# Up product of a decoder layer: the four sums of each unit's hidden rows on VectorE instead of GpSimd

## Chip, cores and metric

The kernel runs on one core of one Trainium2 chip. The metric is the device time of one launch in microseconds (us), the median over several runs; lower is better.

## What is computed

One layer of a decoder trunk for 2048 prompt tokens and 64 sample tokens (8 sequences of 8), model width 1024, hidden width 4096, all in float32. After the mixer (sparse attention and a gated recurrence) comes the part that matters here:

```
x = x + rmsnorm(mix, g_post_mix)
hid = jnp.square(jax.nn.relu(rmsnorm(x, g_pre_mlp) @ w_up))
x = x + rmsnorm(hid @ w_down, g_post_mlp)
```

The change lies in the product with w_up for the prompt rows and its squared ReLU.

## The kernel before

The launch has three stages: projections, attention, and output with MLP. The last one, `output_and_mlp`, does the output product, then the up product, then the down product. Both MLP products for the prompt use Winograd's form of Strassen's scheme: a product of two 2x2 block matrices is made from seven block products P1 to P7 instead of eight, at the price of sums of blocks before and after. Since a fast fp32r matmul has less precision than float32, each operand is split into a high part (a rounding copy on ScalarE) and a low part (raw minus high, on VectorE), and each block product is three passes: high x high, high x low, low x high.

**The up product.** The prompt is cut into two halves (h = 0, 1) of 1024 tokens. Each half has 16 units (f), each of two columns of blocks of w_up, so there are NU = 32 units of NPROD = 7 products, in the order P1, P2, P6, P5, P7, P3, P4; n = 7u + i numbers the products from 0 to 223. A product is 12 matmuls of 128x128 by 128x512 into one of 8 PSUM banks. Its operand on the side of w_up is one piece of 256 KB per product, its operand on the side of the tokens is four pieces (q) of 256 KB that are loaded once per half, in its first unit (unit 0 and unit 16). So `PIECES` lists five pieces per product for units 0 and 16 and one for all others, and `READY_AT[n]` is the count of pieces that product n needs. The raw pieces pass through RAW = 12 buffers (`up_raw`).

Each engine has its own program and they meet by semaphores:

- **SyncE** (its DMA queue is SP) walks the products. For product n it issues loads until piece READY_AT[n] + 12 (`load_up`; each waits until VectorE has made the low part of the piece 12 back, semaphore `lo_rdy`). At i == 4 of unit u it issues the stores of unit u - 1 (`store_hidden(u - 1)`, L3049): seven DMAs of 256 KB to scratch, after a wait for `hid_rdy` and `hsum_rdy`. Loads and stores are in one queue, in this order of the program.
- **ScalarE** makes high parts AHEAD = 5 products ahead (`up_high`, L3255 for tokens, L3260 for w_up), copies P1 out of its bank (`first_out`, L3267), and makes ReLU and square of the four blocks of hidden rows (`square_hidden`, L3272 and L3274, `hid_rdy`).
- **VectorE** does for each n first the low parts of product n + 5 (`up_low`, L3460) and then takes product n out of its bank with Winograd's sums (`out_of_up_bank`, L3479 to L3493).
- **TensorE** (`up`, L3700) waits for the low parts of product n (`lo_rdy`) and for its bank.
- **GpSimd** (`hidden_sums`, L3163 to L3169) makes from the four squared blocks of a unit the four sums that the down product's seven forms need. The hidden rows of even and odd units lie in two buffers, `hidden_even` and `hidden_odd`.

```
                        if u and i == 4:
                            store_hidden(u - 1)
                sp.wait_ge(hs_out[0], 16 * NPROD * NU // 2)
                for m in range(B_RAW, HALF_K):
                    load_b(m)
```

**Into the down product.** The first four pieces of w_down (`load_b`, L3062) are loaded while the last unit runs; pieces 4 to 7 wait until the stores of unit 30 have landed (the two lines above behind the loop). The first hidden rows (`load_a`, L3178) come over GpSimd's queue. The stores of unit 31 stand in SP ahead of the pieces of w_down for the second group of steps; ScalarE makes the high part of the first of these ahead of the hidden rows of the third down step.

Of the kernel before, what the change touches and what calls it, by code (L numbers as in the profile page):

```python
# [22 lines left out]
ALU = mybir.AluOpType  # L23
# [2776 lines left out]
def output_and_mlp(nc, io, sc):  # L2800
# [30 lines left out]
    with ExitStack() as ctx:  # L2831
# [104 lines left out]
        def H(u):  # L2936
            return H_odd if u % 2 else H_even
# [69 lines left out]
        with nc.Block() as block:  # L3007
# [117 lines left out]
            def _(pool):  # L3125
# [28 lines left out]
                        pool.dma_start(sc["xc"][h, i, :, :, own], sums[:, m % 2, s, :].rearrange("p (q t) -> p q t", q=QUADS))\  # L3154
                            .then_inc(xsum_out[m % 2], 16)

                def hidden_sums(u):
                    z = H(u)
                    a11, a12, a21, a22 = z[:, P1, :], z[:, P2, :], z[:, C12, :], z[:, P4, :]
                    pool.wait_ge(hid_rdy, 4 * u + 3)  # L3160
                    if u >= 2:
                        pool.wait_ge(hs_out[u % 2], 16 * NPROD * (u // 2))
                    pool.tensor_tensor(z[:, P5, :], a21, a22, ALU.add).then_inc(hsum_rdy, 1)  # L3163
                    pool.tensor_tensor(z[:, P7, :], a11, a21, ALU.subtract).then_inc(hsum_rdy, 1)
                    pool.wait_ge(hsum_rdy, 4 * u + 1)
                    pool.tensor_tensor(z[:, P6, :], z[:, P5, :], a11, ALU.subtract).then_inc(hsum_rdy, 1)
                    pool.wait_ge(hid_rdy, 4 * u + 4)
                    pool.wait_ge(hsum_rdy, 4 * u + 3)
                    pool.tensor_tensor(z[:, P3, :], a12, z[:, P6, :], ALU.subtract).then_inc(hsum_rdy, 1)  # L3169

                def load_a(s):
                    i, kk, r = STEPS[s]
                    if s >= A_RAW:
# [21 lines left out]
                for n in range(TILES + 2):  # L3195
                    if n >= 3:
                        forms(n - 2)
                    if n < TILES:
                        store_x1(n)
                for u in range(NU):  # L3200
                    if u == NU - 1:
                        pool.wait_ge(mm_done, LAST_UP - 4)
                        for s in range(A_RAW):
                            load_a(s)
                    hidden_sums(u)
                k = 0
                for s in range(len(STEPS)):
                    if s + A_RAW < len(STEPS):
# [212 lines left out]
            def _(dve):  # L3421
# [30 lines left out]
                def up_low(g):  # L3452
# [6 lines left out]
                        high, out = wp[:, n % SLOTS, 0, :], wp[:, n % SLOTS, 1, :]  # L3459
                    dve.tensor_tensor(out, raw[:, g % RAW, :], high.bitcast(F32), ALU.subtract).then_inc(lo_rdy, 1)  # L3460

                def out_of_up_bank(n):
                    u, i = divmod(n, NPROD)
                    z, h = up_bank(n), H(u)
                    if i == P1:
                        return
                    dve.wait_ge(mm_done, n + 1)
                    if i == P2:
                        dve.wait_ge(s1_rdy, u + 1)
                        if u == 0:  # L3470
                            dve.wait_ge(o_sq, 2 * TILES)
                            for b in range(LOAD):
                                dve.wait_ge(x1_out[b], 16 * len(range(b, TILES, LOAD)))
                        elif u == 1:
                            wait_x_stored(dve, 1)
                        else:
                            dve.wait_ge(hs_out[u % 2], 16 * NPROD * (u // 2))
                            dve.wait_ge(hsum_rdy, 4 * (u - 1))
                        dve.tensor_tensor(h[:, P1, :], s1[:, :], z, ALU.add).then_inc(ev, 1)  # L3479
                    elif i == P6:  # L3480
                        dve.tensor_tensor(u2[:, :], s1[:, :], z, ALU.add).then_inc(ev, 1)
                    elif i == P5:
                        dve.wait_ge(ev, NPROD * u + 2)
                        dve.tensor_tensor(u4[:, :], u2[:, :], z, ALU.add).then_inc(ev, 1)
                    elif i == P7:
                        dve.wait_ge(ev, NPROD * u + 3)
                        dve.tensor_tensor(u3[:, :], u2[:, :], z, ALU.add).then_inc(ev, 1)
                        dve.wait_ge(ev, NPROD * u + 4)
                        dve.tensor_tensor(h[:, P4, :], u3[:, :], up_bank(n - P7 + P5), ALU.add).then_inc(ev, 1)
                    elif i == P3:  # L3490
                        dve.tensor_tensor(h[:, C12, :], u4[:, :], z, ALU.add).then_inc(ev, 1)
                    else:
                        dve.tensor_tensor(h[:, P2, :], u3[:, :], z, ALU.subtract).then_inc(ev, 1)  # L3493
# [113 lines left out]
                for n in range(-AHEAD, len(READY_AT)):  # L3607
                    while n + AHEAD < len(READY_AT) and split < READY_AT[n + AHEAD]:
                        up_low(split)
                        split += 1  # L3610
                    if n >= 0:
                        out_of_up_bank(n)
                    if n == LAST_UP - 3:
                        b_low(0)
                        b_low(1)
                    if n == LAST_UP - 2:
                        for m in range(2, 6):
                            b_low(m)
                        a_low(0)
                    if n == LAST_UP - 1:  # L3620
                        b_low(6)
                        b_low(7)
                        a_low(1)

                k = 0
                for s, (i, kk, r) in enumerate(STEPS):
                    if s == 1:
# [270 lines left out]
```

## Time and profile before

| | |
|---|---|
| median of 3 runs | 4140.19 us (4137.55 to 4142.27) |
| the profiled execution, its own time | 4148.16 us |
| its span in the trace | 4146.4 us |
| TensorE busy | 3604.0 us, 87% of the span |
| VectorE busy | 2882.3 us, 70% |
| ScalarE busy | 2206.5 us, 53% |
| GpSimd busy | 924.2 us, 22% |
| mean granted TensorE clock | 0.931 |
| up product | from about 2796 to 3428 us of the span |

Times in rows of the timeline are us from the start of the span. The profiled execution is 1.8 us longer than its span and 8.0 us above the median. A row of the timeline joins like instructions that follow each other: start, time until the end of the last, engine, line, operation, tiles, count, and in brackets the idle time ahead of it and what ended it.

### The profile page before, as it was taken

The numbers are of one execution on the slowest core, as the hardware profiler recorded it, in microseconds if no ns is written. First come the engines' busy times: TensorE is split into PE (matmuls) and PEld (weight loads), VectorE is DVE, ScalarE is ACT, GpSimd is POOL, SyncE is SP. The second block draws the span as 40 slices with busy tenths as digits, with TensorE's granted clock in tenths as the row PEclk, the third lists the DMA queues.
The fourth block names the chain that finished last, engine by engine and source line by source line (L and its number), as shares of the span: only waits on it lengthen the run. The fifth ranks groups of instructions, "written<-read, shape, count | busy, mean of one in ns | idle before, by whom it ended". The sixth has DMA issues, their size and how long they took to land. (4 is left out here: it accounts for less than half of the span.)

```text
span 4146.4 us, 52837 instructions
## 1 busy us (share of the span) xinstructions
PE 3604.0 (87%) x18060; PEld 2870.5 (69%) x18061; DVE 2882.3 (70%) x4890; ACT 2206.5 (53%) x3666; POOL 924.2 (22%) x945
## 2 busy tenths in 40 slices
PE   8999997778877479875399998878999998999998
PEld 7878776667755235444288886767887886888886
DVE  6685665887798788888578885666556554564565
ACT  3343333655677589887477774335455443443232
POOL 0000002554311011100156640343222331000011
PEclk9999998999977799996599999989999999999999
DMA  6555444334300134432456643457668656554464
GB/s 171 170 145 161 137 126 116 94 96 131 92 26 26 51 132 166 160 112 94 133 174 223 224 147 115 163 188 235 197 189 257 194 175 197 181 187 150 137 215 135
DMA packets 487214, 624.48 MB, mean 151 GB/s; under 512 B 97432, under 2 KB 329848, under 8 KB 478648
## 3 DMA queue, kind: packets, MB, share of 16 engines
q1 hardware_dynamic: 424584, 361.25, 29.5%
q0 software_dynamic: 61968, 260.07, 18.6%
q8 instruction: 137, 2.24, 0.2%
q14 instruction: 109, 0.89, 0.1%
q10 hardware_dynamic: 416, 0.02, 0.0%
HBM read 444.45 MB, written 176.77 MB: 150 GB/s over the span
## 5 line engine op out<-in xcount | busy, mean ns | idle before, releaser
L3700 PE MATMUL up_acc<-x_parts_first,w_up_parts 128*128 128x512 f32 x1536 | 357.5, 392 | 26.3 <-DVE w_up_parts L3460 26.3
L712 PE MATMUL accumulated<-hT,w_in_parts 128*128 128x512 f32 x1536 | 356.7, 392 | 0.0
L3700 PEld LDWEIGHTS up_acc<-x_parts_first,w_up_parts 128*128 128x128 f32 x1536 | 290.6, 189 | 87.8 <-DVE w_up_parts L3460 27.2
L2710 DVE TENSOR_SCALAR_CACHE_REDUCE junk_dve<-score,candidate 128x2048 bf16<-128x2048 f32 (+6 forms) x224 | 328.5, 1505 | 8.8 <-DVE candidate L2696 8.3
L3791 PE MATMUL down_acc<-w_down_parts_even,hidden_parts 128*128 128x512 f32 x1344 | 316.4, 393 | 17.8 <-DVE hidden_parts L3497 11.6
L712 PEld LDWEIGHTS accumulated<-hT,w_in_parts 128*128 128x128 f32 x1536 | 288.2, 189 | 60.8
L3791 PE MATMUL down_acc<-w_down_parts_odd,hidden_parts 128*128 128x512 f32 x1344 | 312.7, 390 | 0.0
L3791 PEld LDWEIGHTS down_acc<-w_down_parts_even,hidden_parts 128*128 128x128 f32 x1344 | 254.7, 190 | 72.2 <-issue 19.0
L2633 ACT ACTIVATE junk_act<-score,candidate 128x1920 bf16<-128x1920 f32 (+6 forms) x224 | 285.9, 1287 | 21.0 <-DVEq L2697 16.4
L3791 PEld LDWEIGHTS down_acc<-w_down_parts_odd,hidden_parts 128*128 128x128 f32 x1344 | 251.8, 188 | 53.2 <-issue 1.0
L330 ACT ACTIVATE w_in_parts<-w_in_raw 128x1024 fp32r<-128x1024 f32 (+1 forms) x112 | 113.6, 1014 | 308.9 <-PE accumulated L708 121.7
L3280 ACT ACTIVATE hidden_parts<-hidden_raw 128x1024 fp32r<-128x1024 f32 x112 | 118.6, 1059 | 288.8 <-PE down_acc L3791 288.8
L468 DVE TENSOR_TENSOR w_in_parts<-w_in_raw,w_in_parts 128x1024 fp32r<-128x1024 f32 (+1 forms) x112 | 130.9, 1169 | 195.2 <-ACT w_in_parts L330 194.3
L3460 DVE TENSOR_TENSOR w_up_parts<-up_raw,w_up_parts 128x512 fp32r<-128x512 f32 x224 | 176.8, 789 | 115.0 <-ACT w_up_parts L3260 113.4
L708 PE MATMUL accumulated<-w_in_parts,hT 128*128 128x512 f32 (+1 forms) x1152 | 239.1, 366 | 1.7 <-DVE hT L489 1.7
L2018 DVE TENSOR_TENSOR probs_T<-p_T,probs_T 128x512 fp32r<-128x512 f32 x272 | 183.8, 688 | 76.0 <-ACT probs_T L1939 74.9
L708 PEld LDWEIGHTS accumulated<-w_in_parts,hT 128*128 128x128 f32 x1152 | 200.3, 188 | 31.4 <-issue 1.9
L1296 PE MATMUL dots<-ki_high,qi_parts 128*128 128x512 f32 (+3 forms) x304 | 145.8, 481 | 71.9 <-ACT relu L1318 70.0
L3497 DVE TENSOR_TENSOR hidden_parts<-hidden_raw,hidden_parts 128x1024 fp32r<-128x1024 f32 x112 | 137.0, 1223 | 101.8 <-ACT hidden_parts L3280 101.4
L1939 ACT ACTIVATE probs_T<-p_T 128x512 fp32r<-128x512 f32 x272 | 157.1, 594 | 94.1 <-PE p_T L1876 93.0
L3764 PE MATMUL out_acc<-w_out_parts,mix_T 128*128 128x512 f32 (+1 forms) x816 | 196.2, 400 | 2.0 <-DVE w_out_parts L3578 2.0
L1365 DVE SCALAR_TENSOR_TENSOR score<-relu,wi,score 128x1024 f32<-128x1024 f32 (+7 forms) x154 | 180.4, 1172 | 24.9 <-ACT relu L1318 7.9
(535 smaller groups left out, 8534.2 us busy)
## 6 DMA issues: line engine op xcount, KB each, us to landing
hidden_raw<-scratch_hs POOLq DMA_DIRECT2D x112, 512.0 KB, 4.6
w_in_raw<-in_w_in SPq DMA_DIRECT2D x80, 512.0 KB, 4.1
up_raw<-scratch_ws SPq DMA_DIRECT2D x128, 256.0 KB, 4.1
scratch_hs<-hidden_even SPq DMA_DIRECT2D x112, 256.0 KB, 3.6
scratch_hs<-hidden_odd SPq DMA_DIRECT2D x112, 256.0 KB, 3.7
up_raw<-in_w_up SPq DMA_DIRECT2D x96, 256.0 KB, 4.7
weight_sums<-in_w_down POOLq DMA_DIRECT2D x16, 1024.0 KB, 5.3
scratch_wt<-weight_sums POOLq DMA_DIRECT2D x16, 1024.0 KB, 5.6
```

Source lines behind the costliest of these rows:

```text
L708: mm = pe.matmul(z, h[:, a, k, n * P:(n + 1) * P], w2[:, g % 2, b, k2 * w:(k2 + 1) * w], start=(first and j == 0), stop=(last and j == 2))
L712: mm = pe.matmul(z, w2[:, g % 2, b, k2 * ST + n * P:k2 * ST + (n + 1) * P], h[:, a, k, :], start=(first and j == 0), stop=(last and j == 2))
L1296: pe.matmul(dots[:, u % DB, c:c + w], qs[:, b, h, :], kh[:, k], start=True, stop=False)
L1365: dve.scalar_tensor_tensor(s, r, wi[:, i, h:h + 1], s, ALU.mult, ALU.add).then_inc(acc_done, 1)
L1939: act.activation(ET[:, s % 3, 0, :], pT[:, turn_at[s] % 3, :], ACT.Copy).then_inc(th_rdy, 1)
L2018: dve.tensor_tensor(ET[:, s % 3, 1, :], pT[:, turn_at[s] % 3, :], ET[:, s % 3, 0, :].bitcast(F32), ALU.subtract).then_inc(tl_rdy, 1)
L2633: act.activation(ja[:, n % 2, 0:WIDTH[i]], score[:, SOFF[i]:SOFF[i + 1]], ACT.Sign, bias=cf[:, c:c + 1], accum_out=cnt[:, c:c + 1]).then_i ...
L2710: dve.tensor_scalar(jd[:, n % 2, 0:WIDTH[i]], score[:, SOFF[i]:SOFF[i + 1]], cf[:, c:c + 1], None, ALU.is_ge, ALU.add, accum_out=cnt[:, c: ...
L3460: dve.tensor_tensor(out, raw[:, g % RAW, :], high.bitcast(F32), ALU.subtract).then_inc(lo_rdy, 1)
L3700: mm = pe.matmul(up_bank(n), wp[:, n % SLOTS, b, q * P:(q + 1) * P], X(i)[:, a, q, :], start=(q == 0 and (a, b) == (0, 0)), stop=(q == QUA ...
L3764: mm = pe.matmul(acc[0:rows(n), n % 2, c, :], aT[:, n % 2, a, k, 0:rows(n)], wo[:, k, b, c * ST:(c + 1) * ST], start=(k == 0 and (a, b) == ...
L3791: mm = pe.matmul(down_bank(s), ap[:, s % A_PARTS, a, j * P:(j + 1) * P], B(ph)[:, j, b, :], start=(j == 0 and (a, b) == (0, 0)), stop=(j = ...
```

## The change

`hidden_sums` moves from GpSimd's program into VectorE's, with the same four operations, semaphores and waits. VectorE calls it for unit u - 1 right behind the eviction of P5 of unit u (n % 7 == 3), and for the last unit, 31, behind the whole loop. GpSimd keeps only its loads of hidden rows at that place. ScalarE, TensorE and SP have the same instructions in the same order as before.

```diff
@@ gpsimd
-                def hidden_sums(u):
-                    z = H(u)
-                    a11, a12, a21, a22 = z[:, P1, :], z[:, P2, :], z[:, C12, :], z[:, P4, :]
-                    pool.wait_ge(hid_rdy, 4 * u + 3)
-                    if u >= 2:
-                        pool.wait_ge(hs_out[u % 2], 16 * NPROD * (u // 2))
-                    pool.tensor_tensor(z[:, P5, :], a21, a22, ALU.add).then_inc(hsum_rdy, 1)
-                    pool.tensor_tensor(z[:, P7, :], a11, a21, ALU.subtract).then_inc(hsum_rdy, 1)
-                    pool.wait_ge(hsum_rdy, 4 * u + 1)
-                    pool.tensor_tensor(z[:, P6, :], z[:, P5, :], a11, ALU.subtract).then_inc(hsum_rdy, 1)
-                    pool.wait_ge(hid_rdy, 4 * u + 4)
-                    pool.wait_ge(hsum_rdy, 4 * u + 3)
-                    pool.tensor_tensor(z[:, P3, :], a12, z[:, P6, :], ALU.subtract).then_inc(hsum_rdy, 1)
@@ gpsimd
-                for u in range(NU):
-                    if u == NU - 1:
-                        pool.wait_ge(mm_done, LAST_UP - 4)
-                        for s in range(A_RAW):
-                            load_a(s)
-                    hidden_sums(u)
+                pool.wait_ge(mm_done, LAST_UP - 4)
+                for s in range(A_RAW):
+                    load_a(s)
@@ vector
+                def hidden_sums(u):
...
+                    dve.tensor_tensor(z[:, P5, :], a21, a22, ALU.add).then_inc(hsum_rdy, 1)
...
@@ vector
                     if n >= 0:
                         out_of_up_bank(n)
+                    if n >= NPROD and n % NPROD == P5:
+                        hidden_sums(n // NPROD - 1)
@@ vector
+                hidden_sums(NU - 1)
                 k = 0
                 for s, (i, kk, r) in enumerate(STEPS):
```

The first place is VectorE from the low parts of product 112 on, where the token pieces of the second half begin (unit 15). Before:

```order
L3460 TENSOR_TENSOR x_parts_first<-up_raw,x_parts_first 128x512 x4
L3460 TENSOR_TENSOR w_up_parts<-up_raw,w_up_parts 128x512
L3484 TENSOR_TENSOR sum_four<-sum_two,up_acc 128x512
L3460 TENSOR_TENSOR x_parts_first<-up_raw,x_parts_first 128x512 x4
L3460 TENSOR_TENSOR w_up_parts<-up_raw,w_up_parts 128x512
L3487 TENSOR_TENSOR sum_three<-sum_two,up_acc 128x512
```

In the changed kernel (L3443 is L3460 of before, L3481 is L3484, L3484 is L3487):

```order
L3443 TENSOR_TENSOR x_parts_first<-up_raw,x_parts_first 128x512 x4
L3443 TENSOR_TENSOR w_up_parts<-up_raw,w_up_parts 128x512
L3481 TENSOR_TENSOR sum_four<-sum_two,up_acc 128x512
L3451 TENSOR_TENSOR hidden_even<-hidden_even 128x512
L3452 TENSOR_TENSOR hidden_even<-hidden_even 128x512
L3454 TENSOR_TENSOR hidden_even<-hidden_even 128x512
L3457 TENSOR_TENSOR hidden_even<-hidden_even 128x512
L3443 TENSOR_TENSOR x_parts_first<-up_raw,x_parts_first 128x512 x4
L3443 TENSOR_TENSOR w_up_parts<-up_raw,w_up_parts 128x512
L3484 TENSOR_TENSOR sum_three<-sum_two,up_acc 128x512
```

Unit 14's sums now stand on VectorE behind the eviction of P5 of unit 15, and the low parts of product 114 (the second row of x_parts_first) stand behind them. The same pattern stands in each of the units 1 to 31.

The second place is VectorE at the end of the up product, in the changed kernel (L3490 takes the last product out of its bank):

```order
L3490 TENSOR_TENSOR hidden_odd<-sum_three,up_acc 128x512
L3451 TENSOR_TENSOR hidden_odd<-hidden_odd 128x512
L3452 TENSOR_TENSOR hidden_odd<-hidden_odd 128x512
L3454 TENSOR_TENSOR hidden_odd<-hidden_odd 128x512
L3457 TENSOR_TENSOR hidden_odd<-hidden_odd 128x512
L3500 TENSOR_TENSOR w_down_parts_odd<-down_raw,w_down_parts_odd 128x512
```

The sums of unit 31 stand between the last eviction and the first low part for the second group of down steps; before, these two followed each other.

## Rows read from the trace of the kernel before

**Rows 1.** The page: the span, and the median landing of hidden stores.
```profile
span 4146.4 us, 52837 instructions
...
scratch_hs<-hidden_odd SPq DMA_DIRECT2D x112, 256.0 KB, 3.7
```

**Rows 2.** Waits of TensorE, 2787 to 3600 us: us in total, times, longest.
```profile
PE up_acc L3700 <- DVE w_up_parts L3460: 31.5, 5, 16.9
```

**Rows 3.** Windows: length, then busy us of PE, PEld, DVE, ACT, POOL; PEclk, DMA.
```profile
3150.00:3169.00 19.00, 19.00 (x85) 15.73 (x84) 14.04 (x18) 11.75 (x21) 10.85 (x8) 1.00 0.87 253
...
3135.00:3142.30 7.30, 7.30 (x25) 5.92 (x26) 5.99 (x10) 1.79 (x3) 0.00 (x0) 0.77 1.00 283
```

**Rows 4.** Groups of the up stage, busy and mean ns; then L3460, 3127 to 3135 us, min/median/max.
```profile
L3163 POOL TENSOR_TENSOR hidden_even<-hidden_even 128x512 f32<-128x512 f32 x16 | 20.7, 1294 | 212.2 <-ACT hidden_even L3274 212.2
...
L3484 DVE TENSOR_TENSOR sum_four<-sum_two,up_acc 128x512 f32<-128x512 f32 x32 | 22.0, 686 | 35.3 <-PE up_acc L3700 35.3
...
L3460 DVE TENSOR_TENSOR x_parts_last<-up_raw,x_parts_last x5: 679/1757/1779, 3127.8 to 3134.8; 128x512 fp32r<-128x512 f32 x5
```

**Rows 5.** Timeline of an ordinary odd-even pair of units, 3160 to 3185 us.
```profile
3161.14 11.04 PE L3700 MATMUL up_acc<-x_parts_first,w_up_parts 128*128 128x512 f32 x48
...
3167.40 5.49 SPq L3049 DMA_DIRECT2D scratch_hs<-hidden_odd  x7
...
3172.22 0.69 DVE L3484 TENSOR_TENSOR sum_four<-sum_two,up_acc 128x512 f32<-128x512 f32 x1 [1.17 <-PE up_acc L3700]
```

**Rows 6.** Timeline of unit 15 and the start of unit 16, 3103 to 3128 us.
```profile
3104.92 5.04 SPq L3049 DMA_DIRECT2D scratch_hs<-hidden_even  x7
...
3109.53 2.49 DVE L3460 TENSOR_TENSOR x_parts_first<-up_raw,x_parts_first 128x512 fp32r<-128x512 f32 x4
...
3110.00 2.70 SPq L3037 DMA_DIRECT2D up_raw<-scratch_xc  x4
...
3112.53 0.68 DVE L3484 TENSOR_TENSOR sum_four<-sum_two,up_acc 128x512 f32<-128x512 f32 x1
...
3115.28 2.59 ACT L3255 ACTIVATE x_parts_first<-up_raw 128x512 fp32r<-128x512 f32 x4 [4.89 <-DMA up_raw<-scratch_xc]
...
3117.81 11.04 PE L3700 MATMUL up_acc<-x_parts_first,w_up_parts 128*128 128x512 f32 x48
...
3118.57 0.69 DVE L3460 TENSOR_TENSOR w_up_parts<-up_raw,w_up_parts 128x512 fp32r<-128x512 f32 x1
```

**Rows 7.** Timeline of unit 16 and the start of unit 17, 3127 to 3146 us.
```profile
3127.84 6.45 DVE L3460 TENSOR_TENSOR x_parts_last<-up_raw,x_parts_last 128x512 fp32r<-128x512 f32 x4
...
3134.95 7.31 PE L3700 MATMUL up_acc<-x_parts_last,w_up_parts 128*128 128x512 f32 x24 [3.38 <-DVE w_up_parts L3460]
...
3139.16 2.71 SPq L3042 DMA_DIRECT2D up_raw<-scratch_ws  x4
...
3141.00 0.68 DVE L3484 TENSOR_TENSOR sum_four<-sum_two,up_acc 128x512 f32<-128x512 f32 x1
...
3143.93 0.69 DVE L3460 TENSOR_TENSOR w_up_parts<-up_raw,w_up_parts 128x512 fp32r<-128x512 f32 x1 [2.25 <-ACT w_up_parts L3260]
```

**Rows 8.** Timeline from the up to the down product, 3414 to 3460 us.
```profile
3414.80 9.28 SPq L3049 DMA_DIRECT2D scratch_hs<-hidden_even  x7
...
3419.74 0.69 DVE L3484 TENSOR_TENSOR sum_four<-sum_two,up_acc 128x512 f32<-128x512 f32 x1 [2.03 <-PE up_acc L3700]
...
3427.65 1.76 SPq L3062 DMA_DIRECT2D down_raw<-scratch_wt  x4
...
3434.10 13.38 PE L3791 MATMUL down_acc<-w_down_parts_even,hidden_parts 128*128 128x512 f32 x48 [6.24 <-issue]
...
3437.08 0.68 DVE L3493 TENSOR_TENSOR hidden_odd<-sum_three,up_acc 128x512 f32<-128x512 f32 x1
...
3442.46 7.78 SPq L3049 DMA_DIRECT2D scratch_hs<-hidden_odd  x7
...
3458.77 4.85 PE L3791 MATMUL down_acc<-w_down_parts_even,hidden_parts 128*128 128x512 f32 x12 [11.30 <-DVE hidden_parts L3497]
```

More of the change, by code:

```diff
@@ L3460, in up_low @@
                     dve.tensor_tensor(out, raw[:, g % RAW, :], high.bitcast(F32), ALU.subtract).then_inc(lo_rdy, 1)
+                def hidden_sums(u):
+                    z = H(u)
+                    a11, a12, a21, a22 = z[:, P1, :], z[:, P2, :], z[:, C12, :], z[:, P4, :]
+                    dve.wait_ge(hid_rdy, 4 * u + 3)
+                    if u >= 2:
+                        dve.wait_ge(hs_out[u % 2], 16 * NPROD * (u // 2))
+                    dve.tensor_tensor(z[:, P5, :], a21, a22, ALU.add).then_inc(hsum_rdy, 1)
+                    dve.tensor_tensor(z[:, P7, :], a11, a21, ALU.subtract).then_inc(hsum_rdy, 1)
+                    dve.wait_ge(hsum_rdy, 4 * u + 1)
+                    dve.tensor_tensor(z[:, P6, :], z[:, P5, :], a11, ALU.subtract).then_inc(hsum_rdy, 1)
+                    dve.wait_ge(hid_rdy, 4 * u + 4)
+                    dve.wait_ge(hsum_rdy, 4 * u + 3)
+                    dve.tensor_tensor(z[:, P3, :], a12, z[:, P6, :], ALU.subtract).then_inc(hsum_rdy, 1)
                 def out_of_up_bank(n):
```

## The prediction

> **What bounds the kernel now.** The page gives the span [rows 1]; the change touches only the up product and the step into the down product, so I read TensorE's waits there first. In the whole up stage it waits for a low part five times, 31.5 us in all, 16.9 of them at its start [rows 2]. Elsewhere it is never idle: in an ordinary window of one unit's length it is busy 19.00 of 19.00 us at full clock, VectorE 14.04 and GpSimd 10.85 [rows 3]. So per unit the bound is TensorE, seven products of 2.72 us (48 matmuls of four products take 11.04 us, [rows 5]), and VectorE has room. What can move the time are places where something is late already: the change of halves at unit 16, where TensorE stood 3.38 us for a low part [rows 7], and the step into the down product, where it stood 6.24 and 11.30 us [rows 8]. At each of them I follow SP, because SP keeps its program order and the moved sums release its stores.
>
> **Cost on VectorE.** Added are 128 operations (4 x 32) of 128x512. GpSimd took 1294 ns for such a one; an operation of VectorE on that shape takes 686 ns, its source in PSUM or not [rows 4], and four in a row 2.49 us [rows 6]. With one link of dependence I take 2.6 us a unit. Nominal work of VectorE per unit is then 14 x 0.69 + 2.6 = 12.3 us of 19: covered by TensorE, and low parts are made five products (13.6 us) ahead. If this cover failed, each us would cost 30 us in all; it is a rival below.
>
> **Gain on VectorE.** Where the sums on GpSimd ran beside low parts, a low part took 1757 ns instead of 679 [rows 4]: at unit 16 four of them took 6.45 us [rows 7] instead of 2.49 [rows 6], and TensorE's 3.38 us stall follows on that. The Trainium skill (SBUF — State Buffer, Who interferes with whom) says that a VectorE operation with two SBUF inputs and a GpSimd operation that reads SBUF exclude each other on one shared port for the whole instruction; these rows agree. By that rule alone the change removes a stall, and that is a rival.
>
> **What the later sums do to SP.** Here I part from it. In an ordinary unit the stores of the unit before begin 6.3 us into the unit (3167.40 against 3161.14, [rows 5]). Now the sums come behind the eviction of P5, 3172.22 + 0.7, plus 2.6: 3175.5, so the stores start 8.1 us later, and all loads behind them too. In an ordinary unit that is hidden: with 12 buffers the piece behind the stores is first read about 30 us into the unit (it belongs to product 7u + 17, whose high part may be written once product 7u + 10 is through, 11 x 2.72 us), and it would land 14.4 + 5.5 + about 5 = 25 us into it. The stores themselves land at 14.4 + 5.5 + 3.7 [rows 1], 23 us in, before the same buffer is written again at 24.5.
>
> At the change of halves it isn't hidden, since there 12 buffers are only 2.4 products.
>
> *Stores of unit 14.* SP has loaded through product 113 when it comes to them; product 114's token pieces stand behind. Before: stores at 3104.92, loads at 3110.00, ScalarE reads at 3115.28 after 4.89 us of waiting for them, last low part ready at 3118.57 + 0.69 = 3119.26 [rows 6]. TensorE needs it two products after 3117.81, at 3123.25: 4.0 us of room. Now: eviction of P5 at 3112.53, sums from about 3112.7 to 3115.3, stores then, 10.4 us later. Everything behind is a chain, load by load, so product 114 is ready at 3129.7: a stall of 6.4 us. Products 115 to 118 come at the pace of their loads and high parts, each later than TensorE by about 1 us; TensorE is through with 118 at about 3148, where it was at 3142.26 before.
>
> *Stores of unit 15.* SP stands at product 116 and has loaded through 120; 121 is behind the stores. Before: its load at 3139.16, its low part ready at 3143.93 + 0.69 = 3144.62 [rows 7], needed at 3147.55 (two products after 3142.10). Now the sums follow the eviction of P5, which was at 3141.00 [rows 7]. It comes 10.4 us later by the chain and 2.7 earlier because the four low parts no longer take 6.45 us (4.0 less, of which 1.3 goes to waiting for ScalarE): 3148.7, sums done 3151.9, seven stores of about 5.4 us, load at 3157.35, and from there 5.46 us as before: 3162.8. TensorE restarts 15.2 us later than before. It stood 9 us before that, and after a stall it runs slowly: after the 3.38 us stall 24 matmuls took 7.31 us at a granted clock of 0.77, that is 1.2 GHz for part of it [rows 7, 3], against 5.6 (half of 11.04 and the tail of the last), 1.7 us lost. The two new stalls each pay this; the first is absorbed by the second. **Term one: 15.2 + 1.7 = +17 us**; as bounds I take 13 (loads that land faster once nothing else runs) and 20.
>
> The Trainium skill (Perfetto Trace Analysis, DMA Optimizations) advises one DMA-capable engine for inputs and another for outputs; it speaks against a change that makes outputs late in a queue of inputs. In this kernel rows 6 already show a load waiting behind stores.
>
> **The step into the down product.** Stores of unit 30 were issued at 3414.80 and the pieces of w_down that wait for their landing at 3427.65, 12.85 us later [rows 8]. Now the sums follow 3419.74: done at 3423.0, 8.2 us later. But the stores ran beside 2.5 MB of first loads (9.28 us to issue instead of 5.5); 8 us later these are over, and issue plus landing should be 5.5 + 3.7 - 0.7 = 8.5 us: pieces at 3431.5, +3.8, and TensorE's restart too, from 3434.10 to 3437.9. Its two steps of 13.38 us end at 3451.3, still inside the next stall. That one hangs on the sums of unit 31: GpSimd ended them at 3442.4 (the stores start at 3442.46, [rows 8]); VectorE starts after its eviction, 3437.08 + 3.8 + 0.6, and ends at 3444.1: +1.7. The stores then took 7.78 us beside two loads of hidden rows, which GpSimd, now free, issues earlier: I take 6.5, between 5.5 and 7.78, so w_down's pieces and the restart of 3458.77 come 0.4 us later. **Term two: +0.4 us**, bounds -0.6 and, with stores of unit 30 that take 12.85 us again, +6.
>
> **Sum.** 17.0 + 0.4 = +17.4 us. Against the profiled execution's 4148.2 us that is 4165.6; it stands 8.0 above the median, so against 4140.2 it gives **4157.6 us**, 0.42% slower. About 0.2%, 8.3 us, is what a measurement can tell from no change.
>
> **Rivals.**
>
> *The port wins, not slower (4133 us).* If product 114's pieces still come in time, TensorE loses nothing there, and the stall of 3.38 us with its 1.7 goes: -5.1; at the end unit 31's sums take 2.6 instead of 5.3 us, about -2. It decides at a delay of the stores of under 4.0 us at unit 15. For it: low parts of 1757 ns. Against: SP's order is unchanged, ScalarE already waits 4.89 us for that load, and my delay is 10.4. Chance 0.07, by a third of it faster than 0.2%, were the port worth more elsewhere.
>
> *Only the second store binds (4147 us).* If the loads behind unit 14's stores catch up (they were issued without waiting, and could land faster), 121 is ready 10.4 us earlier, at 3152.4, 4.9 us after its need, plus 1.7 and 0.4: +7. Against: the chain from load to low part has no slack in rows 6. Chance 0.10.
>
> *The end isn't softened (4162 us).* Unit 30's stores take 12.85 us again: +4.4 more. For: SP issues at a pace that I only infer from other units. Chance 0.17.
>
> *VectorE waits in every unit (about 4187 us).* The buffer of hidden rows is free 23 us into a unit and written at 24.5; a landing some us late stops VectorE and with it the low parts. It would have to eat 11 us of lead. One us per unit is 30 us. Chance 0.04.
>
> *As forecast:* 0.62, its own range 4152 to 4162.
>
> **Range and chances.** 4147 to 4165 takes in the forecast, the third rival, the bounds of both terms and the edge of the second rival. Slower by over 0.2%: 0.62 + 0.17 + 0.04 and 0.02 of the second rival, 0.85. Within 0.2%: 0.08 of the second and 0.05 of the first, 0.13. Faster: 0.02.
>
> **What the profile of the changed kernel would show.** Ordinary windows of 19 us with TensorE busy throughout, VectorE about 12.3, and no low part above 0.7 us: right on the cover and the port. The stores of unit 14 at about 3115 us and a TensorE stall of 6 us two products into unit 16; a second of 9 us two products into unit 17, both behind a load of up_raw; a granted clock under 1 behind each. A restart of the down product about 4 us later relative to the last up matmul, and the next at the same distance as before. I am wrong if the loads of product 114 are issued ahead of the stores or land with room, if the stall stays one of 3 us, or if TensorE has gaps in ordinary units.

## The result, and the profile after

The changed kernel takes 4157.81 us (median of 6 runs, 4150.89 to 4159.79); the kernel before took 4142.47 in the same comparison (6 runs, 4137.55 to 4147.01). The ratio is 1.0035, 95% interval 1.0022 to 1.0048: 15.3 us slower by the medians, 14.5 by the ratio. The forecast was 4157.6, +17.4.

The page of the changed kernel, the parts that answer to [rows 1] and the shares of the engines:

```profile
span 4155.9 us, 52838 instructions
...
PE 3608.8 (87%) x18061; PEld 2872.2 (69%) x18061; DVE 2930.8 (71%) x5018; ACT 2205.2 (53%) x3666; POOL 743.7 (18%) x817
...
L3443 DVE TENSOR_TENSOR w_up_parts<-up_raw,w_up_parts 128x512 fp32r<-128x512 f32 x224 | 154.0, 688 | 139.0 <-ACT w_up_parts L3243 138.9
```

The same group on the page of the kernel before:

```profile
L3460 DVE TENSOR_TENSOR w_up_parts<-up_raw,w_up_parts 128x512 fp32r<-128x512 f32 x224 | 176.8, 789 | 115.0 <-ACT w_up_parts L3260 113.4
```

The low parts take 688 ns each over all 224 pieces of weights, where they took 789. The gain that the sums' leaving was to bring VectorE is there: with 128 operations more, of 0.69 us each, it is busy only 48.5 us longer (2930.8 against 2882.3). TensorE nevertheless waits longer for the low parts. What TensorE waits for in the up product and the step behind it (the view of [rows 2]; us in total, times, longest):

```profile
PE up_acc L3700 <- DVE w_up_parts L3443: 44.5, 7, 16.0
PE down_acc L3791 <- issue: 9.3, 1, 9.3
PE down_acc L3791 <- DVE hidden_parts L3494: 6.1, 2, 5.8
```

44.5 us against 31.5, while the last of the three, 11.30 us at its longest in [rows 8], is down to 5.8. An ordinary window of one unit, and the first stall at the change of halves (columns as in [rows 3]):

```profile
3200.00:3219.00 19.00, 19.00 (x86) 15.73 (x85) 11.48 (x18) 9.27 (x18) 0.00 (x0) 1.00 0.67 200
3125.00:3134.00 9.00, 8.34 (x26) 6.42 (x27) 8.96 (x15) 8.78 (x16) 0.00 (x0) 0.70 1.05 394
```

TensorE is busy 19.00 of 19.00 us with GpSimd at zero and VectorE at 11.48: the added work costs nothing there. At the change of halves something isn't covered. This is TensorE's own timeline from unit 15 on (start, length, then in brackets the idle time before it):

```profile
3094.09 11.04 PE L3700 MATMUL up_acc<-x_parts_first,w_up_parts 128*128 128x512 f32 x48
...
3125.66 7.97 PE L3700 MATMUL up_acc<-x_parts_first,w_up_parts 128*128 128x512 f32 x24 [6.92 <-DVE w_up_parts L3443]
...
3144.04 5.60 PE L3700 MATMUL up_acc<-x_parts_first,w_up_parts 128*128 128x512 f32 x24
3157.96 7.18 PE L3700 MATMUL up_acc<-x_parts_first,w_up_parts 128*128 128x512 f32 x24 [8.32 <-DVE w_up_parts L3443]
3164.98 2.88 PE L3700 MATMUL up_acc<-x_parts_fifth,w_up_parts 128*128 128x512 f32 x12
```

Two products into unit 16 it stands 6.92 us, two into unit 17 8.32 us, and behind each stall 24 matmuls take 7.97 and 7.18 us, not 5.60. In the window behind the first, the granted clock is 0.70, and over the 24 matmuls behind the second it is 0.78: TensorE ran part of each at 1.2 GHz, having stood before it. What is behind the stalls is read on SP and VectorE, in the whole timeline of the same stretch:

```profile
3107.19 0.68 DVE L3481 TENSOR_TENSOR sum_four<-sum_two,up_acc 128x512 f32<-128x512 f32 x1
...
3109.78 0.69 DVE L3457 TENSOR_TENSOR hidden_even<-hidden_even 128x512 f32<-128x512 f32 x1
3110.54 5.04 SPq L3049 DMA_DIRECT2D scratch_hs<-hidden_even  x7
...
3115.62 2.72 SPq L3037 DMA_DIRECT2D up_raw<-scratch_xc  x4
...
3120.68 1.32 ACT L3238 ACTIVATE x_parts_first<-up_raw 128x512 fp32r<-128x512 f32 x2 [14.46 <-DMA up_raw<-scratch_xc]
...
3134.06 2.48 DVE L3443 TENSOR_TENSOR x_parts_last<-up_raw,x_parts_last 128x512 fp32r<-128x512 f32 x4
...
3147.56 5.01 SPq L3049 DMA_DIRECT2D scratch_hs<-hidden_odd  x7
3152.62 2.71 SPq L3042 DMA_DIRECT2D up_raw<-scratch_ws  x4
...
3157.22 0.69 DVE L3443 TENSOR_TENSOR w_up_parts<-up_raw,w_up_parts 128x512 fp32r<-128x512 f32 x1 [9.73 <-ACT w_up_parts L3243]
```

The stores of unit 14 start when its sums are done, the loads of product 114 directly behind them, and ScalarE has stood 14.46 us for these (4.89 in [rows 6]). The same follows with unit 15's stores at 3147.56. The four x_parts_last, 6.45 us in [rows 7], take 2.48.

**Where the 9.5 us of span went.** The span grew from 4146.4 to 4155.9 us. In the profiled executions unit 15 begins at 3094.09, and at 3098.77 before: 4.7 us were gained by then, and more than that before the changed code runs at all: already the first up product starts 5.1 us sooner (2791.16 against 2796.26), so I count this as a difference between executions. From unit 0 to unit 15 the changed kernel is 0.4 us slower. From there two distances carry the rest. They need no common zero:

```
distance                                           before   after   difference
start of unit 15 to start of product 123             54.21    70.89   +16.7
end of the last up matmul to the 24 matmuls
  behind the third down step                         36.06    33.55    -2.5
```

The rows of the kernel before from which they are taken:

```profile
3098.77 11.04 PE L3700 MATMUL up_acc<-x_parts_first,w_up_parts 128*128 128x512 f32 x48
...
3152.98 2.88 PE L3700 MATMUL up_acc<-x_parts_fifth,w_up_parts 128*128 128x512 f32 x12
...
3422.26 5.60 PE L3700 MATMUL up_acc<-x_parts_last,w_up_parts 128*128 128x512 f32 x24
...
3463.92 5.63 PE L3791 MATMUL down_acc<-w_down_parts_even,hidden_parts 128*128 128x512 f32 x24
```

The first ends in each trace at the 12 matmuls on x_parts_fifth in unit 17. The two make +14.2, beside a measured 15.3. I use the same two distances for every experiment.

The end of the up product in the changed kernel, in the timeline that answers to [rows 8]:

```profile
3434.26 5.60 PE L3700 MATMUL up_acc<-x_parts_last,w_up_parts 128*128 128x512 f32 x24
...
3435.10 5.04 SPq L3049 DMA_DIRECT2D scratch_hs<-hidden_even  x7
...
3442.92 1.76 SPq L3062 DMA_DIRECT2D down_raw<-scratch_wt  x4
...
3449.20 13.73 PE L3791 MATMUL down_acc<-w_down_parts_even,hidden_parts 128*128 128x512 f32 x48 [9.34 <-issue]
...
3455.55 5.05 SPq L3049 DMA_DIRECT2D scratch_hs<-hidden_odd  x7
...
3461.55 1.74 SPq L3062 DMA_DIRECT2D down_raw<-scratch_wt  x3
...
3468.70 4.41 PE L3791 MATMUL down_acc<-w_down_parts_even,hidden_parts 128*128 128x512 f32 x12 [5.77 <-DVE hidden_parts L3494]
...
3473.41 5.61 PE L3791 MATMUL down_acc<-w_down_parts_even,hidden_parts 128*128 128x512 f32 x24
```

The first restart comes 3.1 us later after the last up matmul (9.34 against 6.24): unit 30's stores start 8.3 us later, and issuing them takes 5.04 us where it took 9.28. The second comes 2.1 us earlier (28.84 against 30.91): unit 31's stores start 1.1 us later, and issuing them takes 5.05 us where it took 7.78.

### The profile page after: what moved, and what is told of

Read it like the earlier page. It is cut to its first block and busy times, and to the rows that moved or that the text cites. A ratio compares the mean times of both kernels' runs of the same rounds, so it can differ in the third digit from the quotient of the medians.

```text
span 4155.9 us, 52838 instructions
## 1 busy us (share of the span) xinstructions
PE 3608.8 (87%) x18061; PEld 2872.2 (69%) x18061; DVE 2930.8 (71%) x5018; ACT 2205.2 (53%) x3666; POOL 743.7 (18%) x817
## 5 line engine op out<-in xcount | busy, mean ns | idle before, releaser
L3164 POOL DMA_DIRECT2D hidden_raw<-scratch_hs x112 | 59.3, 529 | 1185.2 <-PE up_acc L3700 615.0
L3443 DVE TENSOR_TENSOR w_up_parts<-up_raw,w_up_parts 128x512 fp32r<-128x512 f32 x224 | 154.0, 688 | 139.0 <-ACT w_up_parts L3243 138.9
L708 PEld LDWEIGHTS accumulated<-w_in_parts,hT 128*128 128x128 f32 x1152 | 200.3, 188 | 31.5 <-issue 1.9
```

The source lines that it names most:

```text
L708: mm = pe.matmul(z, h[:, a, k, n * P:(n + 1) * P], w2[:, g % 2, b, k2 * w:(k2 + 1) * w], start=(first and j == 0), stop=(last and j == 2))
```

## The experiments

My theory: the 16.7 us are SP's program order. The stores wait for sums that are made later, and the loads of the next products stand behind them. Rivals: VectorE's added work itself, and a hidden cost in all the other units. Every version computes the whole result.

### The stores behind the loads

The changed kernel, but SP comes to the stores of units 14 and 15 after it has issued more loads. Sums, their engine and their time stay.

```diff
-                        if u and i == 4:
+                        if u not in (0, 15, 16) and i == 4:
                             store_hidden(u - 1)
+                        if (u, i) == (16, 1):
+                            store_hidden(14)
+                        if (u, i) == (17, 1):
+                            store_hidden(15)
```

> The changed kernel with one edit: SP issues the stores of unit 14 after it has loaded through piece READY_AT[113] + 12 (unit 16, i = 1) and those of unit 15 after the loads for unit 17, i = 1. VectorE still makes all sums one unit later. My theory (loads stand behind late stores in SP's queue at the change of halves): the stall of 6.9 us and that of 8.3 us go. Left are short stalls at products 116 to 118, about 3 us in all, since the stores of unit 14 still stand between loads, and no slow clock behind them; with the 2.5 us won at the end that gives about 4 us less than the kernel before, 4138, ratio 0.999. Rival (the sums as work on VectorE make the low parts late): SP's order changes nothing, the stalls stay, 4155 to 4160.

Measured: 4140.37 us (12 runs) beside 4142.92 of the kernel before (24 runs); ratio 0.9995 (0.9986 to 1.0003). The whole slowdown is gone. TensorE's timeline at the change of halves in this version:

```profile
3092.54 11.04 PE L3704 MATMUL up_acc<-x_parts_first,w_up_parts 128*128 128x512 f32 x48
...
3126.71 3.01 PE L3704 MATMUL up_acc<-x_parts_last,w_up_parts 128*128 128x512 f32 x12 [1.10 <-DVE w_up_parts L3447]
3130.97 3.02 PE L3704 MATMUL up_acc<-x_parts_last,w_up_parts 128*128 128x512 f32 x12 [1.25 <-DVE w_up_parts L3447]
...
3144.70 2.88 PE L3704 MATMUL up_acc<-x_parts_fifth,w_up_parts 128*128 128x512 f32 x12
```

SP begins unit 14's stores at 3109.04, 16.50 us into unit 15, no earlier than in the changed kernel (16.45). Only the loads stand elsewhere, and both long stalls are gone. The distance is 52.16 us, 2.05 less than before the change. No low part runs beside GpSimd's sums here, but SP's order isn't that of the kernel before either, so no run shows by itself what the low parts gain when GpSimd no longer adds beside them. The same sums on the same engine at the same time cost 18.7 us less here than in the changed kernel (70.89 - 52.16), so VectorE's work isn't their price.

### GpSimd's sums, made late

The kernel before, with GpSimd waiting for the eviction behind which VectorE has the sums in the changed kernel (but for unit 31). It separates when from where.

```diff
                     if u >= 2:
                         pool.wait_ge(hs_out[u % 2], 16 * NPROD * (u // 2))
+                    if u < NU - 1:
+                        pool.wait_ge(ev, NPROD * (u + 1) + 3)
```

> The kernel before with one edit: GpSimd keeps the sums but waits, for units 0 to 30, until P5 of the next unit has been evicted (the point at which VectorE makes them in the changed kernel). My theory (what costs is when the stores are released, not who adds): as slow as the changed kernel and more, because four sums take 5.3 to 5.7 us on GpSimd and 2.6 on VectorE: both stalls 3 us longer, and the restart of the down product 6 us later with stores that end 3 us later; 4142 + 17 + 6 + 3, about 4168, between 4160 and 4172. Rival (it is VectorE's extra work): nothing is added to VectorE, so 4142, ratio within 0.2% of 1.

Measured: 4184.84 us (4 runs), ratio 1.0094 (1.0079 to 1.0109), so +41.9 by the medians. Late sums on GpSimd are slower than late sums on VectorE; the direction is the theory's, the size lies well over the 4160 to 4172 that I wrote down. At the change of halves:

```profile
3138.99 7.35 PE L3702 MATMUL up_acc<-x_parts_first,w_up_parts 128*128 128x512 f32 x24 [12.19 <-DVE w_up_parts L3462]
...
3174.59 8.02 PE L3702 MATMUL up_acc<-x_parts_first,w_up_parts 128*128 128x512 f32 x24 [11.35 <-DVE w_up_parts L3462]
```

The distance is 80.29 us, +26.1. GpSimd ends its four operations later than VectorE: the stores of unit 14 start at 3124.25, 22.1 us into unit 15 and not 16.45. Only about half of these 5.6 us is GpSimd's slower adding (5.2 us for the four against 2.7). The rest is a delay of VectorE, whose eviction of P5 comes 15.95 us into the unit and not 13.10: in this version VectorE stands 23 times in the up product, 48 us in all, until the stores of a buffer of hidden rows have landed. TensorE doesn't notice it before unit 16; there it lengthens the first stall. Both stalls grow, to 12.19 and 11.35, where I had expected 3 us more for each. At the end of the up product another +11.6 came, more than I had put down for it. The timeline of SP and GpSimd there:

```profile
3454.74 1.56 POOL L3171 TENSOR_TENSOR hidden_even<-hidden_even 128x512 f32<-128x512 f32 x1
...
3456.24 1.64 POOL L3180 DMA_DIRECT2D hidden_raw<-scratch_hs  x3
3456.37 7.69 SPq L3049 DMA_DIRECT2D scratch_hs<-hidden_even  x7
...
3468.65 1.76 SPq L3062 DMA_DIRECT2D down_raw<-scratch_wt  x4
...
3475.01 13.43 PE L3793 MATMUL down_acc<-w_down_parts_even,hidden_parts 128*128 128x512 f32 x48 [17.68 <-issue]
```

GpSimd's own loads of hidden rows stand behind its sums in its own order. In the changed kernel they went out at the last products of unit 31; here they go out with the stores, which then take 7.69 us to issue, and w_down's pieces come 12.28 us behind the stores' start where they came 7.82 behind. The stores themselves start 3.8 us later than in the changed kernel, measured from the last up matmul. So the rival "the end isn't softened" does exist, but with the sums on GpSimd.

### Two units' sums back on GpSimd

The changed kernel with the sums of units 14 and 15 made by GpSimd as before (it gets the function back, and calls it for these two).

```diff
-                    if n >= NPROD and n % NPROD == P5:
+                    if n >= NPROD and n % NPROD == P5 and n // NPROD - 1 not in (14, 15):
+                        if n // NPROD - 1 == 16:
+                            dve.wait_ge(hsum_rdy, 64)
                         hidden_sums(n // NPROD - 1)
```

> The changed kernel with the sums of units 14 and 15 alone back on GpSimd, as soon as their squares are ready; all others stay on VectorE. My theory: the two stores are as early as before, so the change of halves costs what it did before (a stall of 3.4 us with low parts of 1.7 us beside the sums of unit 15); the end keeps its 2.5 us: 4140, ratio 0.9995. Rival (VectorE's work in all units): 30 of 32 units are unchanged, so nearly the whole loss stays, about 4156.

Measured: 4141.73 us (12 runs), ratio 0.9994 (0.9986 to 1.0003). Thirty of 32 units on VectorE cost nothing that can be measured; two of them are the whole loss. What the two engines cost each other side by side shows without the late stores, in the timeline of unit 16:

```profile
3125.75 1.30 POOL L3164 TENSOR_TENSOR hidden_odd<-hidden_odd 128x512 f32<-128x512 f32 x1 [24.17 <-ACT hidden_odd L3274]
...
3126.29 6.37 DVE L3460 TENSOR_TENSOR x_parts_last<-up_raw,x_parts_last 128x512 fp32r<-128x512 f32 x4
...
3133.18 2.48 DVE L3460 TENSOR_TENSOR x_parts_last<-up_raw,x_parts_last 128x512 fp32r<-128x512 f32 x4
```

Four low parts take 6.37 us beside GpSimd's sums and 2.48 right after them. That gives a stall of 4.47 us and slow matmuls behind it, and a distance of 56.76: 4.6 more than the 52.16 of the first experiment. It is also 2.6 more than in the kernel before, which I hadn't expected. Unit 13's sums are still on VectorE, so SP issues its stores and the loads behind them late, until just ahead of unit 14's stores. These begin 6.15 us into unit 15, as before, but take 6.70 us to issue and not 5.04, and everything behind them comes 1.7 us later.

### VectorE's work increased

The changed kernel, with each low part of the weights made twice in units 2 to 12 and 18 to 29 (the second overwrites the first with the same values).

```diff
+                    if kind == "w" and (1 < h * FPAIRS + x < 13 or 17 < h * FPAIRS + x < 30):
+                        nonlocal twice_n
+                        dve.tensor_tensor(out, raw[:, g % RAW, :], high.bitcast(F32), ALU.subtract).then_inc(twice, 1)
+                        twice_n += 1
+                        dve.wait_ge(twice, twice_n)
                     dve.tensor_tensor(out, raw[:, g % RAW, :], high.bitcast(F32), ALU.subtract).then_inc(lo_rdy, 1)
```

> The changed kernel; VectorE makes each low part of the w_up pieces of units 2 to 12 and 18 to 29 twice (161 more operations of 0.69 us, each with a wait for itself). VectorE is then busy some 17 of 19 us in those units. My theory (in ordinary units the sums are covered by TensorE's five products of lead): no change against the changed kernel, 4158, at most 3 us more. Rival (ordinary units have no room on VectorE): each added us shows, up to 5.5 us times 23 units, 4280; a tenth of that would already show as 4170.

Measured: 4156.32 us (6 runs), ratio 1.0032 (1.0020 to 1.0044), where the changed kernel has 1.0035. Two ordinary windows:

```profile
3200.00:3219.00 19.00, 19.00 (x85) 15.73 (x84) 16.96 (x28) 10.26 (x19) 0.00 (x0) 1.00 0.75 225
3219.00:3238.00 19.00, 19.00 (x86) 15.72 (x85) 16.07 (x26) 9.27 (x17) 0.00 (x0) 1.00 0.67 191
```

VectorE is busy 16.96 and 16.07 of 19 us, and TensorE doesn't notice. A single window of 19 us can hold operations of its neighbours, so I take 200 us of the timeline (2850 to 3050): VectorE is busy 168.6 us there and 119.9 in the changed kernel, 4.6 us more a unit. The ordinary units cover the 2.7 us that the change added, and 4.6 on top of that.

### Only the last two units on VectorE

The kernel before with the sums of units 30 and 31 alone on VectorE (in this and the next versions a set says which units stay on GpSimd; both engines have the function, and each waits for the other's sums where they change over).

```diff
+    ON_GPSIMD = set(range(30))
```

> The kernel before, with only the sums of units 30 and 31 on VectorE (unit 30's behind the eviction of P5 of unit 31, unit 31's behind the loop, as in the changed kernel). My theory (the two places are independent): the change of halves is as before, with its stall of 3.4 us; at the end the down product starts 3.1 us later and the third step 2.1 us earlier, as in the changed kernel: 28.8 us from the last up matmul to the third down step, where it was 30.9. 2 us less than before, 4141, ratio 0.9995. Rival (the end came early in the changed kernel because of what the change of halves did to the clock or to the queues): 30.9 us again, 4143.

Measured: 4140.41 us (11 runs) beside 4143.32 (26 runs); ratio 0.9992 (0.9983 to 1.0001). The change of halves is as before (54.24), and the end 34.90, -1.2. TensorE at the end of the up product:

```profile
3425.47 13.42 PE L3812 MATMUL down_acc<-w_down_parts_even,hidden_parts 128*128 128x512 f32 x48 [9.40 <-issue]
3445.04 5.46 PE L3812 MATMUL down_acc<-w_down_parts_even,hidden_parts 128*128 128x512 f32 x12 [6.15 <-DVE hidden_parts L3515]
```

A stall of 9.40 us and one of 6.15, as in the changed kernel (9.34 and 5.77): the end's own part of the change is no loss. That it is a gain rests on the 1.2 us of one trace; the measured ratio alone doesn't tell it from no change.

### Only the units at the change of halves on VectorE

```diff
+    ON_GPSIMD = set(range(31)) - {14, 15}
```

> The kernel before, with only the sums of units 14 and 15 on VectorE, one unit later. My theory (two stores behind which token pieces stand make the whole loss): the change of halves costs 16.7 us more than before, the end is as before: 4160, ratio 1.004. Rival (the loss is spread over the units): 2 of 32 units give at most a tenth of it, 4144.

The edit is wider than that text says: unit 31's sums are on VectorE in this version too. Measured: 4155.84 us (10 runs), ratio 1.0034 (1.0025 to 1.0044). The change of halves is 71.14, +16.9:

```profile
3124.17 8.37 PE L3721 MATMUL up_acc<-x_parts_first,w_up_parts 128*128 128x512 f32 x24 [6.44 <-DVE w_up_parts L3462]
...
3157.03 7.36 PE L3721 MATMUL up_acc<-x_parts_first,w_up_parts 128*128 128x512 f32 x24 [8.58 <-DVE w_up_parts L3462]
```

Two units bring the whole loss at the change of halves (8 operations of 128), with the changed kernel's stalls. The end is 32.31, -3.8: unit 30 on GpSimd has its stores out early (stall 6.82), and unit 31 on VectorE ends its sums sooner.

### A version without the late stores

So the best place of the sums differs by unit: GpSimd for unit 14 and unit 30, whose stores something soon waits for, and VectorE for the others, with unit 15's stores behind the loads.

```diff
+    ON_GPSIMD = {14, 30}
...
-                        if u and i == 4:
+                        if u not in (0, 16) and i == 4:
                             store_hidden(u - 1)
+                        if (u, i) == (17, 1):
+                            store_hidden(15)
```

> The changed kernel, with the sums of units 14 and 30 back on GpSimd as soon as their squares are ready, and the stores of unit 15 moved in SP behind the loads for unit 17, i = 1. My theory: unit 14's stores are early again, so product 114 is in time; unit 15's sums no longer run beside low parts and its stores no longer stand ahead of product 121: no stall above 1.5 us and no slow clock, 4 us less than before. At the end the first restart is as in the kernel before (a stall of 6.2 us), and the second comes 4.5 us earlier, since VectorE ends unit 31's sums 2 us earlier and SP issues their stores in 5 instead of 7.8 us. Together 8.5 us less than before, 4134, ratio 0.998. Rival (the stalls only move to the next late piece): as the kernel before, 4143.

Measured: 4134.69 us (11 runs), ratio 0.9983 (0.9974 to 0.9992), 8.6 us faster than the kernel before. Halves 51.86 (-2.3; 4 had been expected), end 30.97 (-5.1).

### And the last store behind the loads

The same, and SP comes to unit 31's stores inside the down product's loop, behind the loads of w_down.

```diff
-                store_hidden(NU - 1)
...
                     if HALF_K + s < HALF_K * PHASES:
                         load_b(HALF_K + s)
+                    if s == 2:
+                        store_hidden(NU - 1)
```

> The kernel of e7 with one more edit: in SP the stores of unit 31 come behind the loads of the first three pieces of w_down of the second group (in the third step of the down loop) instead of ahead of them. My theory (the stall of 11.3 us before the third down step hangs on these stores and nothing else): that stall and the slow clock behind it go, 7 to 9 us less than e7: 4126, ratio 0.996. Rival (something else is late there, the hidden rows of the third step or the sums themselves): no change against e7, 4134.

Measured: 4124.26 us (5 runs, 4120.59 to 4129.04), ratio 0.9954 (0.9941 to 0.9968), 19 us faster than the kernel before and 33 faster than the change. It is 10.4 us below the last version, where 7 to 9 had been expected; 8.3 of them are at the end of the up product. SP and TensorE at the step into the down product:

```profile
3423.58 3.60 SPq L3063 DMA_DIRECT2D down_raw<-scratch_wt  x3
3432.08 5.43 SPq L3050 DMA_DIRECT2D scratch_hs<-hidden_odd  x7
```

```profile
3425.73 15.48 PE L3815 MATMUL down_acc<-w_down_parts_even,hidden_parts 128*128 128x512 f32 x60 [6.88 <-issue]
...
3441.51 5.60 PE L3815 MATMUL down_acc<-w_down_parts_even,hidden_parts 128*128 128x512 f32 x24
```

w_down's pieces go out 8.5 us before the stores and not behind them; the second stall, 11.30 us in [rows 8], has all but gone (0.3), 60 matmuls run on, and the end is 22.66 us, -13.4. The same cure works at a second place.

**All together.** The two distances against the kernel before, and the difference of the medians (us):

```
version                                halves    end     sum   measured
the change                              +16.7   -2.5   +14.2     +15.3
stores behind the loads                  -2.1   -1.7    -3.8      -2.6
GpSimd's sums late                      +26.1  +11.6   +37.7     +41.9
units 14, 15 back on GpSimd              +2.6   -2.2    +0.3      -1.2
VectorE's work increased                +16.4   -2.4   +14.0     +13.4
last two on VectorE                      +0.0   -1.2    -1.1      -2.9
14, 15 and 31 on VectorE                +16.9   -3.8   +13.2     +12.5
14 and 30 on GpSimd, one store late      -2.3   -5.1    -7.4      -8.6
the same, and the last store late        -2.3  -13.4   -15.7     -19.1
```

Two places account for the measured differences to within 2 us in seven of nine and to 4.2 in the others; each distance is from one execution.

## Why the prediction was right

**Cover in ordinary units.** VectorE at 11.48 us (12.3 said), TensorE without a gap from unit to unit, and the work-increasing version shows the cover to be ample. VectorE does wait for a buffer of hidden rows now, as the rival "VectorE waits in every unit" had it: 0.84 us at 3181.30, a unit after the change of halves. It never reaches TensorE. In the second experiment it came in most units, 48 us in all, and in ordinary units TensorE still had no gap: the lead of the low parts covered it.

**Term one, +17: measured +16.7.** The chain, in us from the start of unit 15, the predicted instants being the forecast's less 3098.77:

```
                                     predicted   measured
stores of unit 14 start                  16.5      16.45
product 114 restarts TensorE             30.9      31.57
TensorE through with product 118         49.2      49.95
unit 15's sums done                      53.1      53.4
load behind unit 15's stores             58.6      58.53
product 121 restarts TensorE             64.0      63.87
stall before it                           9         8.32
lost to the slow clock                    1.7       1.6
```

The first instant is right by luck in part. The prediction let the sums begin at 3112.7, while the eviction that they follow lasted until 3113.2 in [rows 6]: by its own rule the stores would have started half a us later. The eviction then came 0.66 us earlier in the unit than before (13.10 us into it, not 13.76), a small gift of GpSimd's leaving that the sum didn't have.

The rival "only the second store binds" fell on its condition: the loads behind unit 14's stores didn't catch up, the first stall is 6.92 us. "The port wins" had its cause (6.45 to 2.48 us for four low parts) and not its effect: where the stores are out of the way the distance is 2.1 to 2.3 us shorter than before, not the 5.1 that the rival gave it, since short stalls at products 116 to 118 stay (0.41 to 1.25 us each); where they aren't, nothing is gained. By the Trainium skill's rule (SBUF — State Buffer, Who interferes with whom) alone the change would have been a gain; the trace agrees with the rule and shows the change's cost elsewhere.

**Term two, +0.4: measured -2.5.** This is the step that was mis-sized, and the rival that made it worse by another 4.4 us fell on its condition: unit 30's stores didn't take 12.85 us again, w_down's pieces went out 7.82 us behind their start. The mechanism stood (first restart later, +3.1 where +3.8 was said; the second hanging on unit 31's stores), four sizes didn't. Unit 31's stores start 1.1 us later, not 1.7. They take 5.05 us to issue: I had taken 6.5, between 5.5 and 7.78, for loads that would run beside them, and in the trace nothing slowed them. The pieces of w_down reach ScalarE 3.17 us after their issue, 0.6 less than the 3.8 that I had carried over. The matmuls behind the stall take 4.41 us, not 4.85. Together 0.6 + 1.45 + 0.6 + 0.4 = 3.0, where 2.9 are to be explained. The last of the four is scatter: the same 12 matmuls take 4.41 to 5.46 us over the versions that keep this stall.

**Sum.** 17.0 + 0.4 was forecast, 16.7 - 2.5 = 14.2 found in one execution, 15.3 measured. The predicted 4157.6 lies 0.2 us from the median, closer than its own steps, and that is luck: the kernel before was 2.3 us above its first median in the comparison, and that made up for the 2.1 us by which the effect was overrated.

**The queue rule.** The prediction weighed the Trainium skill's advice (Perfetto Trace Analysis, DMA Optimizations) of one engine for inputs and another for outputs. What one queue for both can cost is measured here, 16.7 us. But a second queue wasn't needed: with inputs and outputs still on the one queue, two calls moved in its order took the harm away. And in the second experiment a second queue, GpSimd's, blocked its own loads behind its own sums.

**Open.** The stall of 6.2 to 6.9 us at the first restart of the down product remains in the best version; with unit 30's sums on VectorE it is 9.3 to 9.4 (the change and the first, third, fourth and fifth experiments). What it would take to close it wasn't tried, nor the 16 us at the start of the up product. The 5.1 us by which the first up product starts sooner I put down to the execution; no run isolates it. What the low parts gain when GpSimd no longer adds beside them is in no run by itself: the kernel before with only the stores behind the loads wasn't measured.

## What to carry to other kernels

When an operation is moved later, follow what it releases, and then everything that stands behind that in its issuing engine's program order: here 8 of 128 moved operations cost all of the 16.7 us, through stores that held up loads. Slack is to be read at the changes of phase, where buffers cover fewer steps (2.4 products' worth at this one), not in the steady state, where even 4.6 us more of work a unit was free. And an output whose data come late belongs in the queue behind the inputs that don't depend on it: moving one such call took the time from 4134.7 to 4124.3 us, with no work saved at all.

## What the runs showed of the hardware

- Issuing the same seven stores of 256 KB takes SP 5.0 to 6.2 us in the up product, 6.70 right behind a late run of loads (third and seventh experiment), 7.69 to 7.97 beside two or three loads of hidden rows, and 9.28 to 9.88 beside the first loads of the down product. I had expected the difference at the end to shrink, not to go away entirely.
- Four subtractions of 128x512 on VectorE take 2.48 us alone and 6.37 to 6.45 beside GpSimd's sums; the mean of one over the 224 pieces of weights is 789 ns before the change and 688 after.
- In the up product, after stalls of 0.25 to 2.33 us the next 12 matmuls take 3.0 to 3.1 us, nearly the 2.88 of undisturbed ones, and the granted clock is 1.00 in the six of these stretches that were read (both kernels and the first experiment). After stalls of 3.4 to 12.2 us, 24 of them take 7.0 to 8.5, not 5.6, at a granted clock of 0.66 to 0.80 where it was read. The time lost varies (1.4 to 2.9 us) with no order in the length of the stall.
